# Experts' input half of a two-block layer: own token vector read from PSUM, head exponentials moved, last four activations kept on chip, one-hot tables in pairs

## The reference

```python
def block(xi):                                   # xi: normalised tokens
    q = (xi @ w_q).reshape(n, 8, 2, 128)
    s = einsum('nhpc,hpkc->nhpk', q, sub_keys)   # 8 heads, 2 sides, 128 keys
    ts, ti = top_k(s, 16)
    cand_s = ts[:, :, 0, :, None] + ts[:, :, 1, None, :]      # 256 sums of a head
    best_s, best_p = top_k(cand_s, 16)
    idx = ...                                    # expert = 128 * row + slab
    gate = softmax(best_s)
    act = gelu(einsum('nd,nhkd->nhk', xi, u[idx]))            # exact gelu
    return einsum('nhk,nhkd->nd', gate * act, v[idx])
```

## Time and profile before

| | |
|---|---|
| median of three runs | 2632.72 us |
| profiled execution, its own time | 2629.15 us |
| its span, first to last instruction | 2627.4 us |
| PE, PEld busy | 2411.2 (92%), 1331.1 (51%) |
| DVE, ACT, POOL busy | 1802.5 (69%), 1061.0 (40%), 642.5 (24%) |
| first head's query copied out | 517.2 us from the start |
| transposes of the indices | 983.3 |
| first gate matmul, last one's copy | 1015.5, 1227.8 |
| first value slab's matmuls | about 1291 |

### The profile page before, as it was taken

How to read it: one execution, slowest core, us unless ns; L and a number is a source line. 1 busy time by engine, 2 the same in 40 slices (tenths; PEclk the granted TensorE clock), 3 DMA queues, 4 the chain that set the end, 5 groups by cost and what they waited for, 6 DMA issues and landing times.

```text
span 2627.4 us, 36768 instructions
## 1 busy us (share of the span) xinstructions
PE 2411.2 (92%) x12966; PEld 1331.1 (51%) x12966; DVE 1802.5 (69%) x2961; ACT 1061.0 (40%) x1495; POOL 642.5 (24%) x482
## 2 busy tenths in 40 slices
PE   7997767989999957999799999998899999999998
PEld 3344444455555535777455555555344444444454
DVE  5317686549999996886688888875744346777235
ACT  4245322456665644444333333333342224333134
POOL 0002241148977753111422222200300000000001
PEclk9996777999999988999899999999999999999999
DMA  4200001248987766888999999961323322233221
GB/s 164 73 17 0 0 1 64 89 149 279 308 272 262 263 206 204 314 316 316 365 386 366 374 373 369 366 231 53 116 73 112 105 94 91 96 104 104 91 94 49
DMA packets 169938, 480.02 MB, mean 183 GB/s; under 512 B 17728, under 2 KB 75968, under 8 KB 168928
## 3 DMA queue, kind: packets, MB, share of 16 engines
q1 hardware_dynamic: 113664, 293.92, 32.8%
q0 software_dynamic: 36864, 134.23, 14.5%
q10 hardware_dynamic: 19296, 50.34, 4.8%
HBM read 426.00 MB, written 52.43 MB: 182 GB/s over the span
## 4 chain that ended last, share of the span: by engine, by line
PE 68%; DVE 22%; ACT 3%; DMA 2%; issue 2%; DVEq 2%; POOL 1%; SPq 0%; ACTq 0%; POOLq 0%
PE psum L517 20%; PE psum L518 20%; PE psum L519 20%; DVE arena L1912 6%; DVEq L1838 2%; PE psum L407 1%; PE psum L1009 1%; PE psum L1010 1%; DMA arena<-in_w 1%; DVE arena L638 1%; DVE arena L491 1%; PE psum L829 1%; PE psum L869 1%; DVE arena L1849 1%; DVE arena L1851 1%
## 5 line engine op out<-in xcount | busy, mean ns | idle before, releaser
L517 PE MATMUL psum<-arena 128*128 128x384 f16 (+3 forms) x3648 | 1266.4, 348 | 65.6 <-DVE arena L448 13.2
L518 PE MATMUL psum<-arena 128*128 128x384 f16 (+3 forms) x3648 | 1268.4, 348 | 0.0
L519 PE MATMUL psum<-arena 128*128 128x384 f16 (+3 forms) x3648 | 1261.2, 347 | 0.0
L517 PEld LDWEIGHTS psum<-arena 128*128 128x128 f16 (+1 forms) x3648 | 355.7, 98 | 401.5 <-issue 72.8
L519 PEld LDWEIGHTS psum<-arena 128*128 128x128 f16 (+1 forms) x3648 | 354.6, 97 | 326.5 <-issue 11.9
L518 PEld LDWEIGHTS psum<-arena 128*128 128x128 f16 (+1 forms) x3648 | 355.1, 98 | 314.1 <-issue 11.7
L491 DVE SCALAR_TENSOR_TENSOR arena<-arena 128x1024 f16<-128x1024 f32 x216 | 268.4, 1244 | 340.7 <-ACT arena L478 340.1
L478 ACT ACTIVATE arena<-arena 128x1024 f16<-128x1024 f32 x216 | 226.7, 1051 | 285.3 <-PE psum L519 252.2
L1459 ACT ACTIVATE arena<-arena 128x1024 f16<-128x1024 f32 x128 | 135.3, 1057 | 303.1 <-PE psum L519 297.9
L497 POOL TENSOR_TENSOR arena<-arena 128x1024 f16<-128x1024 f32 x104 | 220.0, 2115 | 93.4 <-ACT arena L486 91.9
L2202 POOL DMA_INDIRECT arena<-in_v,arena x128 | 133.7, 1044 | 371.2 <-DVE arena L1923 318.6
(11 more groups left out here) (250 smaller groups left out, 2260.0 us busy)
## 6 DMA issues: line engine op xcount, KB each, us to landing
arena<-in_w SPq DMA_DIRECT2D x320, 512.0 KB, 3.6
arena<-in_v SPq DMA_DIRECT2D x128, 512.0 KB, 6.1
early_activations<-arena ACTq DMA_DIRECT2D x128, 192.0 KB, 4.7
gate_matrix<-arena ACTq DMA_DIRECT2D x6, 4096.0 KB, 16.7
arena<-gate_matrix SPq DMA_DIRECT2D x32, 768.0 KB, 8.4
arena<-early_activations SPq DMA_DIRECT2D x128, 192.0 KB, 6.7
arena<-in_xT SPq DMA_DIRECT2D x4, 512.0 KB, 6.5
arena<-in_urows,arena POOLq DMA_INDIRECT x128, 6.5
```

Of the source, the lines that this page charges most:

```text
L517: nc.tensor.matmul(ps, a_h, b_h, start=first, stop=False)
L518: nc.tensor.matmul(ps, a_h, b_l, start=False, stop=False)
L519: return nc.tensor.matmul(ps, a_l, b_h, start=False, stop=last)
```

## The change

- `own_tok`: PE's transposes leave the own tokens' vectors in banks 6 and 7. Before, ACT copied them to SBUF (two activations); now the dots read them in PSUM and the two copies are gone. The two sums get a place each. The index transposes go to banks 2, 3 and 0 instead of 2, 3 and 6.
- `gate_exp` of head h moves from behind the second woven score copy of turn h+1 to the front of ACT's turn h+1; the last head's moves from behind the second gap slab to the front of the gap.
- The activations of slabs 124 to 127 stay in `act_p`; they are neither stored nor loaded again.
- `QUAD` goes from 4 to 2: a one-hot table is `[4 groups, 128, 2]` and a token's numbers stand 4 bytes apart.
- `LEAD` goes from 12 to 8: the four own adds of slabs 124 and 125 move to the end of the adds (group 29).
- SP's last four input slabs and the first four value slabs are issued in turn instead of the values first.

```diff
-QUAD = 4
+QUAD = 2
+SPILLED = NK - GRP
-TURN_BANKS = (2, 3, 6)
+TURN_BANKS = (2, 3, 0)
-LEAD = 12
+LEAD = 8
...
-        own_tok = r.take(D)
-        own_sum = [own_tok, r.take(D)]
+        own_tok = psum[:, 6 * 512:8 * 512]
+        own_sum = [r.take(D) for _ in range(2)]
...
             sp.wait_ge(g_done, GT * OCT * 2)
-            for s in range(GRP):
-                sp.dma_start(vraw[:, s, :], io["v"][s]).then_inc(vslab_in[s], 16)
-            slabs(N_U + TAIL_AT // SLOTS * SLOTS + 2 * SLOTS, N_POOL)
+            for s in range(SLOTS):
+                n = N_U + TAIL_AT // SLOTS * SLOTS + 2 * SLOTS + s
+                sp.wait_ge(low_cut, n + 1 - SLOTS)
+                sp.dma_start(wraw[:, s, :], io["w"][n]).then_inc(slab_in[s], 16)
+                if s:
+                    sp.dma_start(vraw[:, s - 1, :], io["v"][s - 1]).then_inc(vslab_in[s - 1], 16)
+            sp.dma_start(vraw[:, GRP - 1, :], io["v"][GRP - 1]).then_inc(vslab_in[GRP - 1], 16)
...
-                    for tk in range(QUAD):
+                    for tk in range(OCT // 2):
                         ps = bank(2 * b + half, P, tk * P)
-                        row, high, low = (x[b][:, half, :, tk] for x in (hot_row, hot_high, hot_low))
+                        j = half * (OCT // 2) + tk
+                        row, high, low = (x[b][:, j // QUAD, :, j % QUAD] for x in (hot_row, hot_high, hot_low))
...
             for h in range(PH):
                 m, n = 2 * h, N_PQ + TURN * h
+                if h:
+                    gate_exp(h - 1)
...
-                if h == 0:
-                    act.wait_ge(own_turned, 1)
-                    for half in range(2):
-                        nc.scalar.activation(own_tok[:, half * 512:(half + 1) * 512], bank(6 + half),
-                                             ACT.Copy).then_inc(own_acted, 1)
...
-                    if j == 1 and h:
-                        gate_exp(h - 1)
...
             for e in range(WOVEN, WOVEN + GAP):
+                if e == WOVEN:
+                    gate_exp(PH - 1)
                 spilled(e)
-                if e == WOVEN + 1:
-                    gate_exp(PH - 1)
...
-                if e >= NK - GRP:
-                    for pick in range(2 * (e - NK + GRP) + 4, 2 * (e - NK + GRP) + 6):
+                if e >= NK - 2:
+                    for pick in range(2 * (e - NK) + 8, 2 * (e - NK) + 10):
```

More of the change, by code:

```diff
@@ L237, in build @@
         act_p = v3(r.take(4 * ND), 4)
-        own_tok = r.take(D)
-        own_sum = [own_tok, r.take(D)]
+        own_tok = psum[:, 6 * 512:8 * 512]
+        own_sum = [r.take(D) for _ in range(2)]
         own_at, own_gate, own_dot, own_coef = r.take(PICKS, u32), r.take(PICKS), r.take(PICKS), r.take(PICKS)
         own_rows = v3(r.take(ROWS_G * D), ROWS_G)
-        assert r.at <= WORDS and own_tok.shape[1] + region_g + 2 * P * NT + 4 * ND <= WORDS - 5300
+        assert r.at <= WORDS
         r = Region(region_g)
@@ L320, in build @@
         gmat = nc.dram_tensor("gate_matrix", [GT, P, NK * NT], f32, kind="Internal").ap()
-        early = nc.dram_tensor("early_activations", [NK, P, ND], f32, kind="Internal").ap()
+        early = nc.dram_tensor("early_activations", [SPILLED, P, ND], f32, kind="Internal").ap()
         class Chain:
@@ L689, in load_group @@
                             "a p n -> p (a n)")).then_inc(vslab_in[s], 16)
[L690 to L693, removed]
+                    if acts:
+                        if not first:
+                            sp.wait_ge(gated_out, g * GRP + (s + 1 - GRP))
+                        sp.wait_ge(act_stored[s], g * 16 + 16)
+                        sp.dma_start(act_s[:, s, :], early[bass.ds(g * GRP + s, 1)].rearrange(
+                            "a p n -> p (a n)")).then_inc(act_in[s], 16)
             load_group(0, 0, first=True)
@@ L697, in _ @@
             load_group(1, 1)
-            with sp.Fori(1, GROUPS // 2) as o:
+            with sp.Fori(1, GROUPS // 2 - 1) as o:
                 load_group(o * 2, 0)
                 load_group(o * 2 + 1, 1)
+            load_group(GROUPS - 2, 0)
+            load_group(GROUPS - 1, 1, acts=False)
             sp.wait_ge(acc_out, KC)
@@ L1043, in _ @@
             pe.wait_ge(gelu_out, NK)
+            pe.wait_ge(own_dotted, PICKS)
             pe.wait_ge(idxT_out, 3)
@@ L1390, in early_gelu @@
             def early_gelu(e, n, x, b, k, buf=act_p, before=act_p):
-                if not isinstance(e, int) or e > 0:
+                if 0 < e <= SPILLED:
                     store_early(e - 1, (x - 1) % 4, before)
                 act.wait_ge(slab_done, n + 1)
-                wait(act, act_stored[x], k * 16)
+                if e < NK:
+                    wait(act, act_stored[x], k * 16)
                 nc.scalar.activation(buf[:, x, :], bank(b, ND), ACT.Gelu, scale=ISW).then_inc(gelu_out, 1)
@@ L1906, in own_dots @@
             def own_dots(lo, n):
+                dve.wait_ge(own_turned, 1)
                 for k in range(lo, lo + n):
@@ L1990, in value_low, with value_group @@
                                                op0=ALU.mult, op1=ALU.subtract).then_inc(vlow_cut, 1)
-            def value_group(g, par, turn=None):
+            def value_group(g, par, turn=None, acts=act_s):
                 for s in range(GRP):
                     value_low(g, s)
-                    gated(g, par, s)
+                    gated(g, par, s, acts)
                     if turn is not None:
-                        own_add(g * GRP + (s + LEAD), (1 - par) * GRP + s, turn)
+                        own_add(g * GRP + (s + LEAD), par * GRP + s, turn)
                     gated_low(g, s)
```

25 lines of the change are left out of this document (13 added, 12 removed).

## The result

The changed kernel takes 2565.38 us (median of 4 runs, 2562.63 to 2566.07) against 2632.93 (4 runs, 2629.67 to 2633.20): ratio 0.9749, 95% interval 0.9735 to 0.9763. The forecast was 2560.0, range 2546 to 2592. The profiled execution took 2565.69 us with a span of 2563.9, 63.5 less than the span before.

The account below looks back on a forecast made before the run. PE and DVE were both taken as full in the heads, PE as full in the output half. 2629.15 - 44.7 (heads) - 1 (gap) - 20 (pairs) - 4 (handover) = 2559.5; forecast 2560 us, range 2546 to 2592.

Parts of the forecast that it names:

- start of the heads: Before the first query copy of turn 1: 0.5 us less for the two own-token copies gone from ACT.
- heads: Early exponential and dots from PSUM bring DVE to about PE's pace; index transposes at 938.5, was 983.25: -44.7 us.
- gap: From index transposes to first gate matmul, 32.2 us set by four fetches: stays, -1 us (0 to -2).
- tile turns: One-hot tables in pairs: gate matmuls 0.06 us apart instead of 0.12, DVE then sets the turn: -20 us.
- tail: After the last gate matmul, going into the value half: -4 us (-2 to -6).
- rival A: Gate matmuls: pairs do nothing on PE, one element per read whatever the step, or weight load limits; 2579.5 us, chance 0.29.
- Handover: Ahead of the first value slab: two pairs of own adds instead of three, fewer fetches; -4 us (-2 to -6).
- B: Heads give only half: ACT's waits starve POOL's cuts and PE; 24 us on top, 2584 or 2604, chance 0.11.
- C: Tile turns: DVE's one-hot operations fall to one element a cycle in rows of two; +81 us, 2660, chance 0.08.

## Why the prediction was right

The terms, forecast against the profiled executions (us):

```
                     forecast   measured
start of the heads      0        +3.3
heads                 -44.7     -42.8
gap                    -1        -1.3
tile turns            -20       -18.5
tail                   -4        -4.2
sum                   -69.7     -63.5
```

The medians fell by 67.6 us, close to the forecast's 69.7. The range alone would not have told the forecast from rival A, whose 2579.5 lies in it; the stages and the gate matmuls do.

- **Heads.** The mechanism stood on DVE's dots, late behind POOL, and all of it came: the dots lost their stalls, DVE fell below PE's pace, the turns run at 51.14 us (forecast 51.3), and ACT's new wait is nothing, as priced. The price of PSUM as second input was taken at 0.056 us a dot; it is none, 1216 ns for 1219. By the Trainium skill ("VectorE: DVE Perf Modes", TRN2 errata) the estimate was 65 ns more; the dots disagree.
- **What was mis-sized in the heads** is the last head. L1905 was to come 66.5 us after the query copy of head 7 and came after 68.7. MAX8 was 2.3 us earlier than forecast (22.9 us behind the copy, for 25.2), but from there to L1905 it took 45.8 us for 41.2. The forecast had put 4 us on top of 37.2 for POOL at work; 8.6 came. L1884 and L1889, with two SBUF inputs as before, lost 4.0 in four instructions alone, the small ones at 919.56 and 929.52 some 3 more, and the wait for a dot's row 1.0. The stall had been followed to the dots and not to the other operations that now meet POOL. That POOL is the cause of theirs too is read from the traces, where the small ones end with its cuts and the pairs are free without them (2.36 us each); no run was made for it. Two errors partly cancel here: MAX8 came early by 2.3 us, the rest late by 4.6.
- **The start.** 0.5 us were credited for the two own-token copies; the first query copy of turn 1 came 47.5 us after that of turn 0, as before. The 3.3 us of the start lie within the 6.5 us by which executions differ there.
- **Tile turns.** 0.12 to 0.06 us as forecast, then DVE as the bound. DVE's window says 39.21 of 40 us: the turn, 32.25 us on average, is DVE's 32.04 and its friction. The bound on DVE, not on PE, made the term: 768 x 0.06 = 46 us of PE's time went, and 18.5 were paid out. The Trainium skill ("SBUF — State Buffer", box on cachelines) has a stride as free while two accesses hit each 16-byte line; here 8 bytes cost twice as much as 4, so the rule doesn't hold for these operands, and rival A falls with it.
- **Handover.** -4.2 in one execution, 2.4 on the means of several; the mechanism (a pair of own adds less) is only argued, since the edits were not run apart.
- **Rivals.** A and B fell, C is true at rows of one. B shows what the sum rests on: alone, the early exponential is worth 9.8 us in the heads, since ACT then waits for a DVE that is behind.

## What to carry to other kernels

Where two engines run a hair apart in pace, compare their paces first: an edit that moves a wait pays by the distance to the next engine, here 51.1 against 56.4 us, and only as long as the faster one stays the faster. Follow a stall to every instruction of its kind, not only to those on which it shows now. And a wait for one transfer in a stretch where the DMA engines are full may be a bill for all of them: here two other orders brought nothing. A wait for rows in the gap, where the DMA engines had room (share 0.68 from 944.0 to 974.7 us of the changed kernel), could be filled with work, for 11.8 us.

## What the runs showed of the hardware

- The start-to-start time of an f16 matmul with 128 columns and its weight load depends on the distance of its elements in SBUF: 0.056 us at 2 bytes, 0.06 at 4, 0.12 at 8, 0.23 at 16, so about in proportion from 4 bytes on, at the four distances tried. Both operands have the distance here; which of them costs was not tried. The weight load's own median is 98, 97, 118 and 145 ns.
- A VectorE comparison of f16 with a broadcast row takes 684 ns for 1024 elements in rows of two and of four, 689 in rows of eight, and 1219 in rows of one.
- PE with operands at 16 bytes' distance ran without idle time, and its granted clock was 0.82 on average; at 8 bytes it was 0.99 with PE busy 208.84 of 212 us, and at 4 bytes 1.00 in the tile window shown above, where PE had idle time.
- A VectorE operation with two SBUF inputs, 1.2 us alone, took up to 3.0 us as a dot, and up to 3.7 in other lines, beside a GpSimd subtraction of 2.0 us; with one input in PSUM the dots never passed 1224 ns. Small operations were hit as well, one with a single SBUF input: 1.33 us for 0.18.
- The same code ahead of the heads took 516.2 to 522.7 us in fourteen executions. A single trace's instant is known to no better than that. The heads repeated to 0.1 us in ten kernels; the tail, with code alike, varied by 4.8 us in the four executions with the new tail.
